# The values product of the mixers' attention, and its drain, put a quarter of a job later

## The chip, the cores and the metric

The kernel runs on one core of a Trainium2 chip. The metric is the device time of one execution in microseconds; the median of three runs of the kernel before is 2228.06 us (2226.67 to 2229.28).

## What is computed

Two networks follow each other on 256 rows of width 1024. The first block (dilated and block attention, a cross attention to a memory, a gated MLP with a short convolution) is not touched by the change. The second has two layers. Each layer's mixer takes a normalised input, multiplies it by one wide weight `w_in` and makes three branches of it: an attention, a gated spatial mix, and a convolution of 31 taps. Their gated sum is multiplied by `w_out`. The attention is this, eight query heads of width 128 on two key and value heads:

```python
def gqa_attend(q, k, v):
    s = jnp.einsum('bqhgd,bkhd->bhgqk', q, k).astype(jnp.float32) * ATTN_SCALE
    p = jax.nn.softmax(s, axis=-1).astype(v.dtype)
    return jnp.einsum('bhgqk,bkhd->bqhgd', p, v)
```

It runs three times: for the context rows in layer 0 (256 keys: "context mixer"), and for the main rows in layers 0 and 1 (512 keys, the context's and their own: "main mixers"). All inputs and outputs are float32, and weights are multiplied as a sum of two parts (below).

## The kernel before

**Jobs and quarters.** All weight products are cut into jobs: one job multiplies a 1024 x 512 piece of a weight by 256 rows, in four quarters of 256 weight rows. For each quarter SyncE loads the piece (`raw`), ScalarE (ACT) rounds it to `whi` (L1376), VectorE (DVE) writes the rest `wlo = raw - whi` (L1862), and TensorE (PE) multiplies: high by high, high by low and low by high, into the accumulator `gps` (two job-sized halves that alternate). Lines 1060 to 1062 are a job of the type with 512-wide products, 12 per quarter; lines 1067 to 1069 the other type. The split of quarter q of the next job waits until PE has used quarter q of this one (`used[q]`), so ACT and DVE work a whole job ahead of PE with the weights.

**Steps.** Everything else hangs on the jobs as steps. `put(job, q, kind, ...)` in `make_plan` hangs a step on quarter q of a job. Every engine walks the jobs in order, each quarter in order, and does its own part of each step. PE does the steps of a quarter, then the quarter's products. ACT and DVE do the steps of a quarter, then in the last quarter the job's evacuation from `gps`, then the split of the same quarter of the next job. DVE's steps of the kinds in `LATE` (among them `conv`, one tap of the convolution, four L1705, and `gv_rms`, ten short operations L1677 to L1429) come behind the split. Nothing is reordered at run time, so what stands first in an engine's list holds up what stands behind it.

**The attention in the mixer.** `hosts` in `mixer` names nine consecutive jobs (`ga1`, `gg1`, `gv0`, `gv1`, `gu0`, `gu1`, `gate0`, `gate1`, `branch0`). Job h of them takes the scores of head h, and finishes head h-1. The steps of one head are:

- `at`: PE's scores (L970, L971, in the context mixer L973) into banks 0 and 1 of `aps`; DVE's maximum (L1661, L1662).
- `atE`: ACT's exponential from the banks (L1206). `atR`: DVE's reciprocal of the sums (L1668). `atS`: ACT's scaling of the probabilities (L1215).
- `atT`: PE's transposes of them (L982) into banks 2 and 3 of `aps`, in the next job; ACT's copy to `PTb` (L1223).
- `atV`: PE's product of the values with `PTb` (L995), into bank 2 of `aps`. It waits for the copy.
- `atH`: ACT rounds the result out of bank 2 to `ohi` (L1227). `atL`: DVE writes the rest to `olo` (L1672). `atL` is the last reader of bank 2.

`use` keeps who has to be through with a bank before it is written again. For bank 2 after `atV` that is `atL` of the same head:

```python
            elif k == "atT":
                use(p, (2, 3), ("at_pt", p.of, 1, 1))
            elif k == "atV":
                use(p, (2,), ("at_lo", p.of, 1, 1))
```

and `atT` of the next head begins on PE with `free(p)`, which waits for it.

Of the kernel before, what the change touches and what calls it, by code (L numbers as in the profile page):

```python
# [41 lines left out]
HD2, QH, KVH = 128, 8, 2  # L42
# [57 lines left out]
def make_plan():  # L100
# [10 lines left out]
    def put(jb, q, kind, **args):  # L111
        p = Step(kind, **args)
        jb.aux[q].append(p)
        return p
# [141 lines left out]
    def mixer(l, s, t_h, slots, tab=None, kvc=None, first=None):  # L256
# [58 lines left out]
        hosts = [ga1, gg1, gv[0], gv[1], gu[0], gu[1], gates[0], gates[1], ba[0]]  # L315
        at, tq = [], [tq0]
        for h in range(QH + 1):

            t, e = (0, 1) if h > 1 else (1, 2)
            if h == 1:  # L320
                put(hosts[h], 0, "atR", of=at[0])
                put(hosts[h], 0, "atS", of=at[0])
            if h < QH:
                p = put(hosts[h], 0 if h else 2, "at", h=h, s=s, own=own, l=l, slot=a_, tk=tk, rq=tq[h // 4])
            if h:
                put(hosts[h], t, "atT", of=at[h - 1])
                put(hosts[h], e, "atV", of=at[h - 1])
                put(hosts[h], 2 if h < QH else 1, "atH", of=at[h - 1])
                put(hosts[h], (3 if h == 1 else 2) if h < QH else 1, "atL", of=at[h - 1])
            if h < QH:  # L330
                put(hosts[h], e if h else 3, "atE", of=p)
                if h:
                    put(hosts[h], 2 if h > 1 else 3, "atR", of=p)
                    put(hosts[h], 3, "atS", of=p)
                at.append(p)
            if h == 2:
                tq.append(put(gv[0], 3, "tq", of=rq1, banks=(0, 1)))
# [78 lines left out]
    t_next = prenorm(d1[1], 2, d2[0], 2, 0, "c", 0, "RA", 0, [("ctx_in", None, 0, 16), ("cp_done", j_q0, 1, 1)])  # L416
    put(d2[1], 1, "gb", src=("g_final",))
    J, co, wo = mixer(0, "c", t_next, (0, 1, 2))

    fin = Step("final", after={"act": [("res_done", d2[1], 1, 1)], "dve": [("res_done", d2[1], 1, 1)]})  # L420
# [8 lines left out]
    last_f2 = f2[-1]  # L429

    J, _, wo = mixer(0, "x", t_next, (2, 1, 0), tab, first=first)
    po_c = Step("po", res="c", wait=last_f2)
    J["kv"].aux[0].insert(0, po_c)
# [10 lines left out]
    f2[-1].then.append(po)  # L444
    t_next = prenorm(kvc, 1, kvc, 3, 1, "x", 0, "RB", 1, po=po)
    J, _, wo = mixer(1, "x", t_next, (1, 0, 2), tab, kvc)
    f10 = job("relu2", "ff11", 0, "W", 1, c=0, out=0)
    t = ffn(1, "x", f10, wo[1], 1, (0, 0, 0))
# [1480 lines left out]
```

## Time and profile before

| | before |
|---|---|
| median of 3 runs | 2228.06 us (2226.67 to 2229.28) |
| profiled execution, its own time | 2226.02 us |
| its span in the trace | 2224.2 us |
| mean granted TensorE clock over the span | 0.985 of full speed |
| PE busy | 2113.8 us (95%) |
| DVE busy | 1666.3 us (75%) |
| ACT busy | 1224.8 us (55%) |

The span runs from the first to the last instruction; the execution's own time is 1.8 us longer. In the rows of the timeline the columns are: start in us, length in us, engine, line, operation, what it writes and reads, and how many were merged; in brackets the idle time just before it on its engine, and what ended it. A wait row names who waited, for whom, the total in us, how often, and the longest. The three stretches of attention lie at about 612 to 733 us (context), 1156 to 1291 us (main, layer 0) and 1729 to 1864 us (main, layer 1).

### The profile page before, as it was taken

Reading aid. Unit: us, or ns where it says so; the run is one execution under the profiler, and the core shown is the slowest. Engines: PE = TensorE matmul, PEld = TensorE weight load, DVE = VectorE, ACT = ScalarE, POOL = GpSimd, SP = SyncE. Lnnn points to the kernel's source line nnn. Section 1 sums busy time; section 2 is a strip of 40 time slices with the busy share of each in tenths; the row PEclk is TensorE's granted clock in tenths of the full one; section 3 lists DMA queues with packets and bytes.
Section 4 is the critical chain, followed back from the end, with each engine's and each line's share of the span. In section 5 each row is a group of like instructions: output and inputs, shape, how many; then the busy total and the mean of one; then the engine's idle time right before and its main releaser. Section 6 shows DMA issues by size and latency. Waiting matters only on the chain.

```text
span 2224.2 us, 30895 instructions
## 1 busy us (share of the span) xinstructions
PE 2113.8 (95%) x12005; PEld 1841.2 (83%) x12005; DVE 1666.3 (75%) x2501; ACT 1224.8 (55%) x1651; POOL 58.8 (3%) x112
## 2 busy tenths in 40 slices
PE   7999989998999999999999999989999999998997
PEld 6777779896887887988887788789878878877996
DVE  6676667777778987766687898675687789976555
ACT  5555654555566446555556644554555675454543
POOL 3000000000000000000000000000000000000000
PEclk9999999999999999999999999999999999998999
DMA  7545775667645445677654444556555544444663
GB/s 254 182 156 181 236 257 169 223 216 227 206 144 159 134 142 161 199 231 242 204 187 133 139 135 143 177 175 191 174 174 171 152 133 133 151 161 143 189 187 117
DMA packets 203809, 394.31 MB, mean 177 GB/s; under 512 B 14007, under 2 KB 16563, under 8 KB 203664
## 3 DMA queue, kind: packets, MB, share of 16 engines
q1 hardware_dynamic: 198368, 381.74, 54.7%
q0 software_dynamic: 5296, 10.60, 1.6%
q8 instruction: 96, 1.57, 0.3%
q14 instruction: 49, 0.40, 0.1%
HBM read 390.98 MB, written 1.30 MB: 176 GB/s over the span
## 4 chain that ended last, share of the span: by engine, by line
PE 79%; DVE 9%; ACT 6%; issue 3%; DMA 2%; DVEq 0%; ACTq 0%
PE gps L1060 14%; PE gps L1062 14%; PE gps L1061 14%; PE gps L1067 9%; PE gps L1069 9%; PE gps L1068 9%; DVE wlo L1862 3%; ACT whi L1376 2%; PE aps L1019 2%; PE aps L864 2%; PE aps L995 1%; DMA raw<-ada_w 1%; PE aps L1026 1%; DVE Yc L1705 1%; PE gps L1054 1%
## 5 line engine op out<-in xcount | busy, mean ns | idle before, releaser
L1862 DVE TENSOR_TENSOR wlo<-raw,whi 128x1024 fp32r<-128x1024 f32 (+1 forms) x728 | 873.4, 1213 | 402.1 <-ACT whi L1376 398.8
L1376 ACT ACTIVATE whi<-raw 128x1024 fp32r<-128x1024 f32 (+1 forms) x728 | 756.6, 1049 | 625.8 <-PE gps L1062 360.7
L1060 PE MATMUL gps<-whi,ohi 128*128 128x512 f32 x1624 | 651.9, 401 | 9.6 <-DVE olo L1733 4.9
L1062 PE MATMUL gps<-whi,olo 128*128 128x512 f32 x1624 | 634.4, 391 | 0.0
L1061 PE MATMUL gps<-wlo,ohi 128*128 128x512 f32 x1624 | 634.0, 390 | 0.0
L1067 PE MATMUL gps<-ohi,whi 128*128 128x256 f32 x1760 | 503.8, 286 | 0.6 <-issue 0.5
L1068 PE MATMUL gps<-olo,whi 128*128 128x256 f32 x1760 | 498.5, 283 | 0.0
L1069 PE MATMUL gps<-ohi,wlo 128*128 128x256 f32 x1760 | 498.4, 283 | 0.0
L1060 PEld LDWEIGHTS gps<-whi,ohi 128*128 128x128 f32 x1624 | 306.3, 189 | 77.3 <-issue 9.7
L1062 PEld LDWEIGHTS gps<-whi,olo 128*128 128x128 f32 x1624 | 305.5, 188 | 65.6
L1061 PEld LDWEIGHTS gps<-wlo,ohi 128*128 128x128 f32 x1624 | 306.1, 188 | 61.3
L1067 PEld LDWEIGHTS gps<-ohi,whi 128*128 128x128 f32 x1760 | 337.6, 192 | 8.5 <-issue 5.5
L1068 PEld LDWEIGHTS gps<-olo,whi 128*128 128x128 f32 x1760 | 337.7, 192 | 0.7
L1069 PEld LDWEIGHTS gps<-ohi,wlo 128*128 128x128 f32 x1760 | 337.5, 192 | 0.0
L1705 DVE SCALAR_TENSOR_TENSOR Yc<-GLP,CW,Yc 128x256 f32<-128x256 f32 x612 | 252.7, 479 | 0.0
L1054 PE MATMUL gps<-whi,chi 128*128 128x512 f32 x192 | 81.4, 424 | 16.7 <-DVE wlo L1862 16.7
L1055 PE MATMUL gps<-wlo,chi 128*128 128x512 f32 x192 | 77.2, 402 | 0.0
L1054 PEld LDWEIGHTS gps<-whi,chi 128*128 128x128 f32 x192 | 37.5, 195 | 30.8 <-DVE wlo L1862 23.8
L864 PE MATMUL aps<-ident,RB 128*128 128x128 f32 x160 | 28.9, 348 | 32.4 <-DVE RB L1448 30.0
L1781 DVE TENSOR_TENSOR TT<-TT 128x1024 f32<-128x1024 f32 x24 | 29.4, 1226 | 37.3 <-ACT TT L1318 37.3
L864 PEld LDWEIGHTS aps<-ident,RB 128*128 128x128 f32 x160 | 24.6, 182 | 36.9 <-DVE RB L1448 33.8
L1206 ACT ACTIVATE Pb<-aps,den,st 128x512 f32<-128x512 f32 (+1 forms) x48 | 33.5, 703 | 32.4 <-DVE den L1662 32.4
(286 smaller groups left out, 1624.1 us busy)
## 6 DMA issues: line engine op xcount, KB each, us to landing
raw<-w_in SPq DMA_DIRECT2D x232, 512.0 KB, 3.8
raw<-w_ff SPq DMA_DIRECT2D x192, 512.0 KB, 4.1
raw<-ada_w SPq DMA_DIRECT2D x96, 512.0 KB, 4.8
raw<-w_out SPq DMA_DIRECT2D x32, 512.0 KB, 4.4
raw<-w_attn_o SPq DMA_DIRECT2D x24, 512.0 KB, 3.3
raw<-w_gmlp_o SPq DMA_DIRECT2D x24, 512.0 KB, 3.3
raw<-w_conv_o SPq DMA_DIRECT2D x24, 512.0 KB, 4.2
raw<-w_gate SPq DMA_DIRECT2D x20, 512.0 KB, 4.4
```

Of the source, the lines that this page charges most:

```text
L864: t = nc.tensor.transpose(aps[:, b, i * S + m * P:i * S + m * P + P], src[:, m, (2 * b + i) * P:(2 * b + i + 1) * P], ident[:])
L1054: mm(o[:, 0:NW], chi[:, k, :], whi[:, q, i, :], start=first, stop=False)
L1055: t = mm(o[:, 0:NW], chi[:, k, :], wlo[:, q, i, :], start=False, stop=last)
L1060: mm(om, ah, whi[:, q, i, :], start=first, stop=False)
L1061: mm(om, ah, wlo[:, q, i, :], start=False, stop=False)
L1062: t = mm(om, al, whi[:, q, i, :], start=False, stop=last)
L1067: mm(on, wh, ohi[:, jb.slot, k, :], start=first and n % 2 == 0, stop=False, skip_group_check=True)
L1068: mm(on, wh, olo[:, jb.slot, k, :], start=False, stop=False, skip_group_check=True)
L1069: t = mm(on, wl, ohi[:, jb.slot, k, :], start=False, stop=last, skip_group_check=True)
L1376: A_(part(whi, jb, q), part(raw, jb, q), ACT.Copy).then_inc(hi_done[q], 1)
L1705: stt(y, x, CW[:, p.l, tap * KT + k:tap * KT + k + 1], y, ALU.mult, ALU.add).then_inc(sem["cv_done"], 1)
L1862: tt(part(wlo, jb, q), part(raw, jb, q), f32(part(whi, jb, q)), ALU.subtract).then_inc(lo_done[q], 1)
```

## The change

Three entries of the table of steps get other quarters. The values product goes from quarter 1 to quarter 2 of its job, ACT's rounding and DVE's rest from quarter 2 to quarter 3. This holds for heads 1 to 6, which are finished in the jobs `gv0` to `gate1`. Head 0 (finished in `gg1`) had its product in quarter 2 already and its rest in quarter 3; only its rounding moves, from 2 to 3. Head 7 (finished in `branch0`) keeps its places. No operation is added or taken away, and no wait is changed.

```diff
             if h:
                 put(hosts[h], t, "atT", of=at[h - 1])
-                put(hosts[h], e, "atV", of=at[h - 1])
-                put(hosts[h], 2 if h < QH else 1, "atH", of=at[h - 1])
-                put(hosts[h], (3 if h == 1 else 2) if h < QH else 1, "atL", of=at[h - 1])
+                put(hosts[h], 2 if h < QH else 1, "atV", of=at[h - 1])
+                put(hosts[h], 3 if h < QH else 1, "atH", of=at[h - 1])
+                put(hosts[h], 3 if h < QH else 1, "atL", of=at[h - 1])
```

DVE in the context mixer, job `gv1`, from its second quarter's split to its evacuation (`L1752`); `L1862` is the split, `L1705` a tap, `L1672` the rest of the values product, `L1668` the reciprocal:

```order
 L1862 TENSOR_TENSOR wlo<-raw,whi 128x1024 x2
 L1705 SCALAR_TENSOR_TENSOR Yc<-GLP,CW,Yc 128x256 x4
-L1672 TENSOR_TENSOR olo<-aps,ohi 128x256
-L1668 RECIPROCAL den<-den 128x2
-L1862 TENSOR_TENSOR wlo<-raw,whi 128x1024
-L1705 SCALAR_TENSOR_TENSOR Yc<-GLP,CW,Yc 128x256 x4
+L1668 RECIPROCAL den<-den 128x2
+L1862 TENSOR_TENSOR wlo<-raw,whi 128x1024
+L1705 SCALAR_TENSOR_TENSOR Yc<-GLP,CW,Yc 128x256 x4
+L1672 TENSOR_TENSOR olo<-aps,ohi 128x256
 L1752 TENSOR_TENSOR TT<-TT,gps 128x1024
```

The rest, last reader of bank 2, now stands behind the third quarter's split and the tap that follows it; the reciprocal stands ahead of both without the rest before it.

ACT in the same job, from the scaling's predecessor to the evacuation (`L1206` exponential, `L1234` another step's squares, `L1376` the rounding of the weights, `L1240` the first tap, `L1227` the rounding of the values product, `L1215` the scaling, `L1298` the evacuation):

```order
 L1206 ACTIVATE Pb,den<-aps,den,st 128x256 x2
 L1234 ACTIVATE RB,st<-RA 128x512 x2
-L1376 ACTIVATE whi<-raw 128x1024
-L1227 ACTIVATE ohi<-aps 128x256
-L1376 ACTIVATE whi<-raw 128x1024
+L1376 ACTIVATE whi<-raw 128x1024 x2
 L1240 ACTIVATE Yc<-GLP,C,CW 128x256 x4
+L1227 ACTIVATE ohi<-aps 128x256
 L1215 ACTIVATE Pb<-Pb,den 128x256 x2
 L1298 ACTIVATE TT<-gps 128x1024
```

The rounding of the product goes behind the third quarter's rounding of weights, and stays ahead of the scaling. On PE the product passes the 12 weight products of the second quarter.

## Rows read from the trace of the kernel before

**Rows 1.** The page: busy time of each engine over the span.
```profile
PE 2113.8 (95%) x12005; PEld 1841.2 (83%) x12005; DVE 1666.3 (75%) x2501; ACT 1224.8 (55%) x1651; POOL 58.8 (3%) x112
```

**Rows 2.** Who waited for whom, PE alone: total, times, longest.
```profile
PE aps L995 <- ACT PTb L1223: 11.7, 10, 1.6
...
PE aps L982 <- ACT Pb L1215: 7.7, 8, 2.3
```

**Rows 3.** Timeline, PE, context mixer: transposes of heads 3 to 7, one product, one head's scores.
```profile
665.84 0.63 PE L982 MATMUL aps<-ident,Pb 128*128 128x128 f32 x4 [0.62 <-ACT Pb L1215]
...
670.80 1.10 PE L995 MATMUL aps<-PTb,kvb 128*128 128x256 f32 x4 [1.57 <-ACT PTb L1223]
...
680.81 0.60 PE L982 MATMUL aps<-ident,Pb 128*128 128x128 f32 x4
...
695.90 0.63 PE L982 MATMUL aps<-ident,Pb 128*128 128x128 f32 x4 [0.38 <-ACT Pb L1215]
...
709.94 1.02 PE L973 MATMUL aps<-kvb,qT 128*128 128x256 f32 x4
...
710.80 0.60 PE L982 MATMUL aps<-ident,Pb 128*128 128x128 f32 x4
...
723.28 0.63 PE L982 MATMUL aps<-ident,Pb 128*128 128x128 f32 x4
```

**Rows 4.** Timeline, PE, main mixer of layer 0: transposes of heads 3 to 7, first scores of head 7.
```profile
1215.73 1.06 PE L982 MATMUL aps<-ident,Pb 128*128 128x128 f32 x8
...
1232.86 1.04 PE L982 MATMUL aps<-ident,Pb 128*128 128x128 f32 x8
...
1248.83 1.06 PE L982 MATMUL aps<-ident,Pb 128*128 128x128 f32 x8
...
1264.13 0.59 PE L970 MATMUL aps<-kvb,qT 128*128 128x256 f32 x2
...
1265.86 1.04 PE L982 MATMUL aps<-ident,Pb 128*128 128x128 f32 x8
...
1280.02 1.07 PE L982 MATMUL aps<-ident,Pb 128*128 128x128 f32 x8 [0.48 <-ACT Pb L1215]
```

**Rows 5.** The rest of the values product by its line: ns of one (min/median/max).
```profile
L1672 DVE TENSOR_TENSOR olo<-aps,ohi x24: 412/417/421, 634.6 to 1861.6; 128x256 fp32r<-128x256 f32 x24
```

**Rows 6.** Timeline, DVE, context mixer: last work of the third quarter, heads 3 to 6.
```profile
665.79 1.67 DVE L1705 SCALAR_TENSOR_TENSOR Yc<-GLP,CW,Yc 128x256 f32<-128x256 f32 x4
...
681.69 0.16 DVE L1429 SCALAR_TENSOR_TENSOR st<-st 128x2 f32<-128x2 f32 x1
...
694.73 1.20 DVE L1862 TENSOR_TENSOR wlo<-raw,whi 128x1024 fp32r<-128x1024 f32 x1
...
710.68 1.66 DVE L1705 SCALAR_TENSOR_TENSOR Yc<-GLP,CW,Yc 128x256 f32<-128x256 f32 x4
```

**Rows 7.** The same for the main mixer of layer 0.
```profile
1215.05 1.67 DVE L1705 SCALAR_TENSOR_TENSOR Yc<-GLP,CW,Yc 128x256 f32<-128x256 f32 x4
...
1232.68 0.16 DVE L1429 SCALAR_TENSOR_TENSOR st<-st 128x2 f32<-128x2 f32 x1
...
1248.36 1.66 DVE L1705 SCALAR_TENSOR_TENSOR Yc<-GLP,CW,Yc 128x256 f32<-128x256 f32 x4
...
1264.30 1.67 DVE L1705 SCALAR_TENSOR_TENSOR Yc<-GLP,CW,Yc 128x256 f32<-128x256 f32 x4
```

**Rows 8.** Timeline, ACT, main mixer: second quarter's rounding in job `gu1`.
```profile
1241.81 1.06 ACT L1376 ACTIVATE whi<-raw 128x1024 fp32r<-128x1024 f32 x1 [0.43 <-PE gps L1062]
```

**Rows 9.** Timeline, ACT, job `gate1`: third quarter's rounding (context; main), scaling (main).
```profile
720.60 1.06 ACT L1376 ACTIVATE whi<-raw 128x1024 fp32r<-128x1024 f32 x1 [1.39 <-PE gps L1062]
...
1276.92 1.06 ACT L1376 ACTIVATE whi<-raw 128x1024 fp32r<-128x1024 f32 x1 [1.39 <-PE gps L1062]
...
1278.54 1.34 ACT L1215 ACTIVATE Pb<-Pb,den 128x512 f32<-128x512 f32 x2 [0.56 <-DVE den L1668]
```

**Rows 10.** A stretch by windows: length, PE, PEld, DVE, ACT, POOL busy, PEclk, DMA share, GB/s.
```profile
2015.00:2030.00 15.00, 4.53 (x20) 3.27 (x19) 10.84 (x28) 5.57 (x10) 0.53 (x1) 0.68 0.54 167
```

## The prediction

> **What bounds the kernel now.** I read the page first: PE is busy for 95% of the span [rows 1], so time comes only from PE's idle time or from other work on PE. Then the waits of PE alone [rows 2]: the values product waits 11.7 us in all for ACT's copy of the transposed probabilities, in ten places, and the transposes wait 7.7 us for ACT's scaling. Then the timeline around such a place. In job `gu0` of the context mixer the transposes start at 665.84 and the product at 670.80, after 1.57 us of idleness [rows 3]. The copy is late because ACT, behind the end of the previous job, has that job's evacuation ahead of it in its list. A product a quarter later would find the copy done. Four of the ten places lie in the context mixer and three in each main one.
>
> Last I read the transposes themselves, the place where one head hands over to the next. They need two things: the scaled probabilities, and bank 2 of `aps`, which the rest of the previous head's product (L1672) must have left. In the trace before, nobody waits for L1672, since it stands ahead of the reciprocal and the reciprocal ahead of the scaling, so it is always done first. That order is what the change gives up.
>
> **What the change removes.** With the product behind the second quarter's 12 weight products (about 2.7 us), all ten waits go: -11.7 us on PE, if nothing else held it. The reciprocal no longer has the 0.42 us of L1672 in front of it [rows 5] (about 0.33 net, because operations on DVE overlap a little), so the scaling can be up to 0.33 us earlier per job where DVE is what it waits for. The rounding on ACT keeps its length and only changes place; it is hidden where ACT idles for PE, as it did for 1.39 us before the rounding of weights in `gate1` [rows 9], and costs up to its 0.4 us where ACT has no slack (job `gv1`, where ACT goes from the weights to the first tap to the scaling). No DMA, SyncE or GpSimd instruction moves.
>
> **What it adds.** The rest now stands behind DVE's third-quarter split and whatever tap or statistics follow it. Its earliest end, counted from ACT's third rounding of weights, which itself waits for PE's third quarter: 1.06 (L1376 [rows 9]) + 1.20 (L1862 [rows 6]) + 1.67 (four L1705 [rows 6]) + 0.42 (L1672 [rows 5]) = 4.35 us; the hops between engines of some 0.1 us (the scaling ends at 1279.88 and the transposes start at 1280.02 [rows 9, 4]) are about made up by the overlap of consecutive DVE operations. PE, from the same moment, has the fourth quarter, 2.62 us (from 1276.92 to 1280.02 less its 0.48 of idleness [rows 9, 4]), and the next head's scores, 1.73 us in a main mixer (1264.13 to 1265.86 [rows 4]) and 0.86 us in the context mixer (709.94 to 710.80 [rows 3]), none before the last transposes. So even when DVE keeps up, PE waits about 0 us per head in the main mixers, 0.8 us in the context mixer, and 1.7 us at the last head of each. Where DVE is behind, it is more.
>
> **The sum, head by head.** The start of the transposes afterwards is the later of PE's arrival and the end of the rest. For the rest I take the end of the DVE work that now precedes it [rows 6, 7], add 0.45, and subtract how much earlier DVE gets there. If it were not earlier at all, the starts of heads 3 to 6 would be:
>
> - Context: 667.9, 682.3, 696.4, 712.8, against 665.84, 680.81, 695.90, 710.80 before [rows 3].
> - Main: 1217.2, 1233.3, 1250.5, 1266.4, against 1215.73, 1232.86, 1248.83, 1265.86 [rows 4].
>
> DVE's lead, from walking through its list and ACT's with the durations of the trace: 0.3 to 0.5 us for heads 3 to 5 of the context mixer and 0.85 us for head 6; in a main mixer 0.6 and 0.5 us for heads 3 and 4, then 1.55 us for heads 5 and 6, because in `gu1` the second rounding of weights waited for PE [rows 8], and PE gets there earlier without the product ahead of it. That gives shifts of the transposes against before of
>
> - context: +1.6, +1.2, 0, +1.15 us for heads 3, 4, 5, 6;
> - main: +0.9, -0.1, +0.1, -1.0 us.
>
> The last head decides, as PE's work behind it is unchanged and PE does not wait there. Its third quarter starts with the shift of head 6, and the transposes follow 4.35 us behind the rounding: context 720.60 + 4.35 = 724.95, main 1276.92 + 4.35 = 1281.27, which is 1.67 and 1.25 us behind the starts before. With head 6: context 1.15 + 1.67 = +2.8 us; main -1.0 + 1.25 = +0.25 us, twice. **Sum +3.3 us.** PE's waits by this: the 11.7 us at the product are gone, some 19 us appear at the transposes, for L1672.
>
> Bounds: the shift of head 6 lies between 0 (PE arriving as before, which the 0.8 us of wait per head nearly forbids) and +2.0 (DVE not earlier) in the context mixer, between -1.4 (PE never held) and +0.5 in a main one. So +1.7 to +3.7, and twice -0.15 to +1.75: +1.4 to +7.2 us. I take 3.3, nearer the low end, because DVE's lead is made of rows that really move up.
>
> Behind the attention DVE is busy without a gap up to the statistics of the convolution, but both engines enter that stretch shifted alike, so I add nothing for it. The granted clock adds noise: long idle stretches of PE, as in 2015 to 2030 us with PE busy for 4.53 of 15 us, are followed by half clock, 0.68 on average there [rows 10], and a shift of the program may lengthen or shorten such a piece; +-2 us.
>
> The profiled execution of 2226.02 us would become 2229.3 us; it lies 2 us under the median of the runs, so the median goes from 2228.06 to **2231.4 us**, +0.15%.
>
> **Rivals.** About 0.2% (4.5 us) is what a measurement of this kernel can tell from no change.
>
> 1. *The waits go and nothing takes their place*: -11.7 us at most. The same walk without the condition on bank 2 gives -1.5 us in the context mixer and twice -3.4 us, because the scaling then holds PE in part: -8.3 us, 2220 us. For it: the largest wait of the attention goes. Against it: `use` gives bank 2 to L1672, and the sum of four operations is longer than the fourth quarter in every one of the last heads. The Trainium skill, page Perfetto Trace Analysis, section Optimization Strategy, says to find the gaps of the engine in question and to make what they wait for start sooner or end faster; read with the wait list alone, this change answers it and would be worth the 11.7 us. Against that rule stands here that the gap is not removed but handed to another dependency. 8%.
> 2. *The forecast: no change that can be told, the sum above*: +1.4 to +4.4 us. 57%.
> 3. *Slower by more than 0.2%*: DVE is the bound of the attention, and its lead stays out. The place is the transposes of heads 3 to 7; if DVE is not earlier, head 6 stands at +2.0 and +0.5, which gives 3.7 + 2 x 1.75 = +7.2 us, 2235 us. It decides from a lead under about 0.4 us less per mixer than I took. For it: nothing in the trace shows how much DVE really gains when PE runs ahead of it, and the longest new wait is large: at head 3 of the context mixer PE arrived at 665.22 before, and by the same walk some 0.9 us earlier now, and is held till 667.4, some 3 us. Were the clock to fall there, the half speed of a few us comes on top. The page TensorE: Matmul & The Clock Gate of the Trainium skill (section Why this matters for your kernels) warns of idle gaps between bursts for this reason; the trace shows full clock over waits of up to 2.3 us in the attention [rows 2] and the half clock only behind longer idleness [rows 10], so 3 us is open. 32%.
> 4. *The product is not what is late*: the copy might still not be there a quarter later. The longest wait is 1.6 us [rows 2] and a quarter's products take 2.7 us, so this is nearly out; 3%, with no change in time.
>
> **The numbers.** The rivals of both signs beyond 0.2%: faster 0.08, slower 0.32; the rest, 0.60 (rivals 2 and 4), is within. The range takes in the bounds of the sum (+1.4 to +7.2 us) and the clock's noise on the low side: 2226.5 to 2236.5 us. It leaves rival 1 out.
>
> **What the changed profile would show.** L995 without idleness before it. L982 waiting for DVE `olo` L1672, about 19 us in 17 or so places, the longest about 3 us at head 3 of the context mixer; its waits for L1215 left only at head 1, where the longest of 2.3 us is. The last transposes of the context mixer about 2.8 us later than before, those of the main mixers 0 to 1 us further behind that. If the transposes wait for L1672 less than 12 us in all, the forecast is wrong towards rival 1; if more than 22 us, towards rival 3.

## The result and the profile after

| | before | after |
|---|---|---|
| median | 2228.06 us (15 runs, 2225.53 to 2234.25) | 2234.37 us (15 runs, 2230.01 to 2237.96) |
| ratio | | 1.0023, 95% interval 1.0014 to 1.0032 |
| profiled execution, its span | 2226.02, 2224.2 us | 2235.13, 2233.3 us |
| mean granted clock | 0.985 | 0.984 |

The change costs 3 to 7 us (the interval times 2228), 5.1 us at the ratio itself; the medians lie 6.3 us apart. A second measurement of the same program, `e8_after_again` below, gave 1.0019 [1.0007, 1.0031]. The predicted 2231.4 us is 3 us too low, and the measured value lies inside the range of 2226.5 to 2236.5 us, nearer its upper end.

The page, busy time over the span, to be held against [rows 1]:

```profile
PE 2119.5 (95%) x12005; PEld 1848.2 (83%) x12005; DVE 1667.2 (75%) x2501; ACT 1224.5 (55%) x1651; POOL 58.6 (3%) x112
```

The same 12005 matmuls are busy for 5.7 us longer. No instruction was added, so a share of PE's work ran slower. The list of PE's waits, against [rows 2]:

```profile
PE aps L982 <- DVE olo L1672: 16.9, 13, 3.0
...
PE aps L982 <- ACT Pb L1215: 5.8, 4, 2.3
```

L995 no longer waits. The 11.7 us before it are gone, and 16.9 us of waits for the rest L1672 stand before the transposes. Of the 7.7 us for the scaling L1215, the 5.8 us that remain are those of heads 0 and 1.

PE in the context mixer: the transposes of heads 0 and 3 to 7, and L1004, the first product of the spatial mix, which stands behind head 7 in `branch0` (against [rows 3]):

```profile
628.18 0.63 PE L982 MATMUL aps<-ident,Pb 128*128 128x128 f32 x4 [2.28 <-ACT Pb L1215]
...
670.36 0.66 PE L982 MATMUL aps<-ident,Pb 128*128 128x128 f32 x4 [2.98 <-DVE olo L1672]
...
686.52 0.66 PE L982 MATMUL aps<-ident,Pb 128*128 128x128 f32 x4 [1.19 <-DVE olo L1672]
...
700.08 0.66 PE L982 MATMUL aps<-ident,Pb 128*128 128x128 f32 x4 [0.22 <-DVE olo L1672]
...
716.16 1.12 PE L982 MATMUL aps<-ident,Pb 128*128 128x128 f32 x4 [2.74 <-DVE olo L1672]
...
731.80 0.66 PE L982 MATMUL aps<-ident,Pb 128*128 128x128 f32 x4 [1.67 <-DVE olo L1672]
...
741.40 0.81 PE L1004 MATMUL aps<-RA,wsT 128*128 128x256 f32 x3
```

The two ends of the same stretch in the kernel before:

```profile
625.05 0.63 PE L982 MATMUL aps<-ident,Pb 128*128 128x128 f32 x4 [2.27 <-ACT Pb L1215]
...
732.86 1.46 PE L1004 MATMUL aps<-RA,wsT 128*128 128x256 f32 x6
```

This distance, from head 0's transposes to L1004, is the measure used from here on, since nothing the change touches lies outside it and the three stretches start at times that vary. In the context mixer it was 732.86 - 625.05 = 107.81 us and is 741.40 - 628.18 = 113.22 us. Read in the same way, a main mixer was 120.90 us (both) and is 120.49 and 120.47 us. Head 0 itself comes 3.1 us later, ahead of everything the change touches: so much do two executions differ there.

What holds the transposes at 670.36 (timeline, DVE and ACT in job `gv1`):

```profile
667.11 0.16 DVE L1668 RECIPROCAL den<-den 128x2 f32<-128x2 f32 x1
667.16 0.37 ACT L1227 ACTIVATE ohi<-aps 128x256 fp32r<-128x256 f32 x1
667.18 1.21 DVE L1862 TENSOR_TENSOR wlo<-raw,whi 128x1024 fp32r<-128x1024 f32 x1
667.42 0.90 ACT L1215 ACTIVATE Pb<-Pb,den 128x256 f32<-128x256 f32 x2
668.30 1.67 DVE L1705 SCALAR_TENSOR_TENSOR Yc<-GLP,CW,Yc 128x256 f32<-128x256 f32 x4
669.88 0.42 DVE L1672 TENSOR_TENSOR olo<-aps,ohi 128x256 fp32r<-128x256 f32 x1
```

The probabilities were scaled at 668.32 and the product rounded at 667.53. On DVE the split (1.21) and the tap (1.67) stand between the rounding and the rest. That is the handing over which the prediction described.

Behind two of these waits PE runs at half clock. The windows behind the waits of 2.98 and 2.74 us (columns as in [rows 10]; the seventh number after the length is the granted clock):

```profile
670.00:675.00 5.00, 4.64 (x16) 3.74 (x17) 4.83 (x7) 2.81 (x4) 0.00 (x0) 0.66 0.46 139
...
716.00:724.00 8.00, 7.84 (x30) 6.57 (x31) 5.33 (x11) 2.87 (x7) 0.00 (x0) 0.79 0.33 114
```

Single products show the change of level (timeline, PE): they start 0.23 us apart at 2.4 GHz, and 0.43 us apart from 671.94 on.

```profile
671.32 0.40 PE L1062 MATMUL gps<-whi,olo 128*128 128x512 f32 x1
671.55 0.59 PE L1060 MATMUL gps<-whi,ohi 128*128 128x512 f32 x1
671.94 0.63 PE L1061 MATMUL gps<-wlo,ohi 128*128 128x512 f32 x1
672.37 0.63 PE L1062 MATMUL gps<-whi,olo 128*128 128x512 f32 x1
```

Such a piece costs 1.5 to 1.6 us: the clock is short of full speed by 0.34 x 5 = 1.7 us of clock time in the first window and 0.21 x 8 = 1.7 in the second, nearly all of it under busy PE. From head 3 to head 4 it is 686.52 - 670.36 = 16.16 us here and 14.56 us in a profile of the same program without the piece (below), from head 6 to head 7 15.64 and 14.16 us.

### The profile page after: what moved, and what is told of

Its sections match the earlier page's. It is cut to its first block, busy times and chain, and to the rows that moved or that the text cites. A ratio compares the mean times of both kernels' runs of the same rounds, so it can differ in the third digit from the quotient of the medians.

```text
span 2233.3 us, 30895 instructions
## 1 busy us (share of the span) xinstructions
PE 2119.5 (95%) x12005; PEld 1848.2 (83%) x12005; DVE 1667.2 (75%) x2501; ACT 1224.5 (55%) x1651; POOL 58.6 (3%) x112
## 4 chain that ended last, share of the span: by engine, by line
PE 75%; DVE 13%; ACT 7%; issue 3%; DMA 3%; DVEq 0%; ACTq 0%
PE gps L1060 13%; PE gps L1061 13%; PE gps L1062 13%; PE gps L1067 9%; PE gps L1068 9%; PE gps L1069 9%; DVE wlo L1862 4%; ACT whi L1376 3%; PE aps L1019 2%; DVE Yc L1705 2%; PE aps L864 2%; DMA raw<-ada_w 2%; PE aps L1026 1%; PE aps L995 1%; PE gps L1054 1%
## 5 line engine op out<-in xcount | busy, mean ns | idle before, releaser
L1862 DVE TENSOR_TENSOR wlo<-raw,whi 128x1024 fp32r<-128x1024 f32 (+1 forms) x728 | 873.8, 1213 | 414.0 <-ACT whi L1376 411.4
L1376 ACT ACTIVATE whi<-raw 128x1024 fp32r<-128x1024 f32 (+1 forms) x728 | 756.5, 1049 | 646.3 <-PE gps L1062 372.2
L1705 DVE SCALAR_TENSOR_TENSOR Yc<-GLP,CW,Yc 128x256 f32<-128x256 f32 x612 | 253.0, 482 | 0.0
L1019 PE MATMUL aps<-GLP,Pb 128*128 128x256 f32 x216 | 51.0, 378 | 0.0
```

The costliest lines, as they stand in the source:

```text
L1019: t = mm(aps[:, i // 2, (i % 2) * S:(i % 2 + 1) * S], Pb[:, p.of.n % 2, i * P:(i + 1) * P], GLP[:, 4 + i, p.of.tap:p.of.tap + S], start=p. ...
L1376: A_(part(whi, jb, q), part(raw, jb, q), ACT.Copy).then_inc(hi_done[q], 1)
L1705: stt(y, x, CW[:, p.l, tap * KT + k:tap * KT + k + 1], y, ALU.mult, ALU.add).then_inc(sem["cv_done"], 1)
L1862: tt(part(wlo, jb, q), part(raw, jb, q), f32(part(whi, jb, q)), ALU.subtract).then_inc(lo_done[q], 1)
```

## The experiments

Theory A: bank 2 is what the transposes wait for. The rest of the product, behind the third quarter's split and a tap, gives it back too late. Theory B: it is the product in its new place, or a later finish of `olo`, that costs. A second question is what the half clock adds. One table holds the stretches of all profiles; "pieces" counts the stretches at half clock within the context mixer's. The main mixers have none but where the table says so. Each kernel is held against the kernel before as measured beside it, whose median lies between 2227.5 and 2229.0 us.

| | ratio to before [95%] | context, pieces | main 0, main 1 |
|---|---|---|---|
| before | 1 | 107.81, 0 | 120.90, 120.90 |
| after | 1.0023 [1.0014, 1.0032] | 113.22, 2 | 120.49, 120.47 |
| after, measured again | 1.0019 [1.0007, 1.0031] | 111.70, 1 | 120.52, 120.54 |
| product moved alone | 0.9969 [0.9958, 0.9981] | 108.39, 2 | 118.09, 118.10 |
| rounding and rest moved alone | 1.0021 [1.0009, 1.0033] | 110.70, 0 | 121.99, 122.05 |
| context product in bank 3 | 0.9981 [0.9972, 0.9990] | 107.49, 2 | 120.45, 120.48 |
| 10 idle products | 1.0019 [1.0009, 1.0029] | 112.57, 0 | 120.45, 120.41 |
| 5 idle products | 1.0009 [0.9996, 1.0022] | 110.11, 0 | 120.52, 120.45 |
| third-quarter taps away | 1.0042 [1.0028, 1.0057] | 113.61, 3 | 124.47, 123.43 (one each) |
| all in quarter 2, rest behind reciprocal | 0.9956 [0.9940, 0.9973] | 107.20, 1 | 116.80, 116.78 |
| rest behind reciprocal alone | 0.9992 [0.9981, 1.0003] | 108.36, 1 | 119.86, 119.88 |
| the last but one, and head 0's wait filled | 0.9958 [0.9945, 0.9970] | 105.72, 0 | 116.79, 116.80 |

### The product alone

Against the changed kernel:

```diff
-                put(hosts[h], 3 if h < QH else 1, "atH", of=at[h - 1])
-                put(hosts[h], 3 if h < QH else 1, "atL", of=at[h - 1])
+                put(hosts[h], 2 if h < QH else 1, "atH", of=at[h - 1])
+                put(hosts[h], (3 if h == 1 else 2) if h < QH else 1, "atL", of=at[h - 1])
```

> The product a quarter later as in the change, its rounding (L1227) and rest (L1672) back in quarter 2, ahead of the reciprocal. Theory A (the late rest holds bank 2, and nothing else of the change costs): the product's wait for L1223 is 0 as after, the transposes' wait for L1672 is gone (16.9 us after), some of it is taken over by the scaling (L1215), net about -1.5 us in the context mixer and -3.4 us in each main one against before: about 2220 us. Rival B (it is the product's later place that costs): as after or worse, 2232 us or more, with waits for the product on ACT and DVE.

Measured: 2221.73 us against 2228.96, ratio 0.9969 [0.9958, 0.9981]. PE's waits at the transposes (this kernel's only row for L982, and none for L995):

```profile
PE aps L982 <- ACT Pb L1215: 13.2, 11, 2.3
```

So the product in its new place costs nothing. By itself it is worth 6.9 us (0.0031 x 2229), and L1672 is waited for by nobody. Where PE waits now, the scaling is what it waits for, the scaling waits for the reciprocal, and the rest stands in front of that (main mixer of layer 0, from the end of job `gu0` to the transposes of head 5):

```profile
1244.48 0.42 DVE L1672 TENSOR_TENSOR olo<-aps,ohi 128x256 fp32r<-128x256 f32 x1
1244.81 0.15 DVE L1668 RECIPROCAL den<-den 128x2 f32<-128x2 f32 x1
...
1245.00 1.33 ACT L1215 ACTIVATE Pb<-Pb,den 128x512 f32<-128x512 f32 x2 [3.05 <-DVE den L1668]
...
1246.48 1.06 PE L982 MATMUL aps<-ident,Pb 128*128 128x128 f32 x8 [1.24 <-ACT Pb L1215]
```

### The rounding and the rest alone

```diff
-                put(hosts[h], 2 if h < QH else 1, "atV", of=at[h - 1])
+                put(hosts[h], e, "atV", of=at[h - 1])
```

> The product in quarter 1 as before, only its rounding and rest late (quarter 3). Theory A: the transposes still wait for L1672, whose time hangs on PE's third quarter and DVE; the product's wait for L1223 is back in part; slower than before by 4 to 9 us, 2232 to 2237 us. Rival B (the product's place costs): no slower than before, 2226 to 2229 us.

Measured: 2233.84 us against 2228.96, ratio 1.0021 [1.0009, 1.0033]. Waits of PE:

```profile
PE aps L982 <- DVE olo L1672: 15.8, 13, 2.3
...
PE aps L995 <- ACT PTb L1223: 3.1, 4, 1.1
```

The loss is there although the product is early: its place does not matter to it, the rest's does. Of the copy's 11.7 us only 3.1 are left with the product where it was. The evacuation still stands ahead of the copy on ACT, but the transposes now come later against it: at head 3 of the context mixer the copy starts 2.7 us behind them (668.25 to 670.98), and 4.2 us in the kernel before (665.84 to 670.08). With the product late as well the total for L1672 is nearly the same, 16.9 us.

### Another bank for the product

In the context mixer the transposes fill bank 2 alone, so its product can go to bank 3 (in the main mixers they fill both). The same index changes in ACT's rounding and in the rest, the order of everything stays that of the changed kernel:

```diff
-                use(p, (2, 3), ("at_pt", p.of, 1, 1))
+                use(p, (2, 3) if p.of.s == "x" else (2,), ("at_pt", p.of, 1, 1))
...
-                use(p, (2,), ("at_lo", p.of, 1, 1))
+                use(p, (2,) if p.of.s == "x" else (3,), ("at_lo", p.of, 1, 1))
```

> The changed kernel, but in the context mixer the product goes into bank 3 of aps, which its four transposes leave free; nothing moves. Theory A: in the context mixer the transposes no longer wait for L1672 (8.8 us there after) and the two stretches of half clock in it go; the scaling holds PE for some of it; 5 to 8 us faster than after, about 2228 us; the main mixers keep 8.1 us of waits for L1672. If the bank is not the cause (DVE too late in general), the time stays within 2 us of after, 2234 us.

Measured: 2225.15 us against 2228.96, ratio 0.9981 [0.9972, 0.9990]. Waits of PE:

```profile
PE aps L982 <- ACT Pb L1215: 9.5, 7, 2.3
PE aps L982 <- DVE olo L1672: 8.1, 8, 1.7
```

The 8.1 us left are the two main mixers'. The rest is as late as before on DVE, and nobody in the context mixer minds: the bank is the cause. The context mixer takes 107.49 us, 5.7 less than in the profile of the changed kernel, with the same number of pieces at half clock. They did not go away as expected: they now lie behind the waits for the scaling at head 0 (2.27 us) and head 5 (1.93 us). The kernel is 9 us faster than the changed one (4.2 + 5.1), where 5 to 8 had been expected; the stretches account for 5.7 of that, and the rest is open.

### The waits filled

Does the half clock come from these waits? On PE, ahead of the transposes of heads 3 and 6 of the context mixer, products with no use into bank 3 keep it busy (10, then 5 in a second kernel):

```diff
             def atT(p):
-                free(p)
                 a = p.of
+                if a.s == "c" and a.h in (3, 6):
+                    wait(pe, p.bank_free[3])
+                    for _ in range(10):
+                        mm(aps[:, 3, 0:S], ident[:], kvb[:, a.own, 0:S], start=True, stop=True)
+                free(p)
```

> The changed kernel with ten more products of 128x256 (identity with keys, into the unused bank 3, nobody reads them) on PE ahead of the transposes of heads 3 and 6 in the context mixer, inside the two longest waits. Theory A with the clock: the transposes start no earlier, their waits there shrink from 3.0 and 2.7 us to under 1 us, no half clock behind them, and the kernel is 3 us faster than after (1.5 us per stretch) though PE does more: 2231 us. If the half clock does not come from these waits: two stretches of half clock remain and the time stays at 2234 us or more.

Measured: 2233.05 us against 2228.96, ratio 1.0019 [1.0009, 1.0029]. No piece at half clock in the context mixer, but ten took over 4 us and outlasted the waits (heads 3 and 6 stand at 43.35 and 88.88 us behind head 0, against 42.17 and 86.36 with five). So it could not tell the price of the clock. Five:

> As e4_fill with five products instead of ten, which lasted 4.2 us there and so outlasted the waits of 3.0 and 2.7 us by 1.2 and 1.5 us. Theory A with the clock: the waits at heads 3 and 6 of the context mixer shrink to 0.9 and 0.6 us, no half clock behind them, the stretch from the first transposes of the context mixer to the spatial product is 3 us shorter than after (113.2 us), 110.2 us. Rival: a remaining wait still brings the half clock, 113 us.

Measured: 2230.96 us against 2227.54, ratio 1.0009 [0.9996, 1.0022]. PE at heads 3 and 6:

```profile
668.90 0.66 PE L986 MATMUL aps<-ident,Pb 128*128 128x128 f32 x4 [0.84 <-DVE olo L1676]
...
713.09 0.65 PE L986 MATMUL aps<-ident,Pb 128*128 128x128 f32 x4 [0.57 <-DVE olo L1676]
```

The context mixer takes 110.11 us: 3.1 less than in the profile of the changed kernel, with over 4 us more of PE's work. That is the price of its two pieces, and 110.1 - 107.8 = 2.3 us is what the order costs there without them. The time alone doesn't show the gain: 2.0 us over the kernel before has an interval of -0.9 to +4.9 us, which overlaps that of the changed kernel.

### The changed kernel again

> The changed kernel once more, for a second profile. The waits for L1672 must be the same to 0.1 us each (16.9 us in all). If the half clock follows from the waits of 2.98 and 2.74 us, both stretches are there again and the context mixer takes 113.2 us from its first transposes to the spatial product; if it is chance, one or both are missing and it takes 111.7 or 110.2 us.

Measured: 2233.19 us against 2227.54, ratio 1.0019 [1.0007, 1.0031]. PE at heads 3 and 6:

```profile
672.51 0.66 PE L982 MATMUL aps<-ident,Pb 128*128 128x128 f32 x4 [3.06 <-DVE olo L1672]
...
716.71 0.66 PE L982 MATMUL aps<-ident,Pb 128*128 128x128 f32 x4 [2.73 <-DVE olo L1672]
```

and the windows behind both (this profile's head 3 lies 2.2 us later than the other's, so its stretch takes a second window):

```profile
670.00:675.00 5.00, 2.49 (x13) 2.15 (x14) 4.82 (x9) 4.50 (x7) 0.00 (x0) 1.00 0.57 177
675.00:686.00 11.00, 10.87 (x49) 8.68 (x47) 8.28 (x19) 7.97 (x16) 0.00 (x0) 1.00 0.45 133
...
716.00:724.00 8.00, 7.29 (x34) 6.14 (x35) 6.81 (x14) 4.21 (x8) 0.00 (x0) 1.00 0.41 139
```

The same program with the same waits has full clock behind both. Its only piece lies behind the wait of 2.27 us at head 0, which the kernel before has too. So a wait of 2 to 3 us brings the half clock in one execution and not in another. Without their pieces, 113.22 - 3.0 and 111.70 - 1.5, both profiles give 110.2 us, as the five idle products did.

This also says that two waits filled and no piece behind them prove little by themselves, since here the same waits stayed unfilled with no piece either. Over all twelve profiles the three attention stretches have 24 unfilled waits of 1.9 us or more at the transposes, with a piece behind 14 of them and no piece anywhere else; the five filled ones (two each in the kernels with 10 and 5 products, and one in the last kernel below) have none.

### The taps out of the rest's way

Theory A puts 1.67 us of tap in front of the rest. Here the third-quarter taps of the host jobs go behind the fourth quarter's split:

```diff
-                    put(J[name], q, "conv", half=half, l=l, of=cv0[half], taps=[tap])
+                    put(J[name], 3 if q == 2 and J[name] in hosts[:QH] else q, "conv", half=half, l=l, of=cv0[half], taps=[tap])
```

> The changed kernel with the convolution's taps that follow the third quarter's split in the eight attention jobs put behind the fourth quarter's, so that only the split (and, in gu0, the statistics) stands ahead of L1672. Theory A (L1672's time is the sum of what stands ahead of it on DVE): the rest ends 1.6 us earlier at heads 3, 6 and 7, and the transposes' waits for L1672 fall from 16.9 us to about 6, mostly at the head of gu0 (1.2 us context, 0.9 us main, nothing moved there); the last wait of each mixer falls from 1.67 to about 0.1 us; 5 us faster than after, 2229 us. Rival B (the product's late place or the bank itself, not what is ahead of the rest): the waits stay, 2234 us.

Measured: 2236.34 us against 2227.54, ratio 1.0042 [1.0028, 1.0057]. The expectation missed. The waits at the last heads did fall (1.67 to 0.78 us in the main mixers), but the total for L1672 stayed at 17.0 us, and main 0 grew by 4.0 us, main 1 by 3.0. DVE at the turn from `gv1` to `gu0` in the main mixer of layer 0, this kernel:

```profile
1229.50 3.25 DVE L1705 SCALAR_TENSOR_TENSOR Yc<-GLP,CW,Yc 128x256 f32<-128x256 f32 x8
1232.67 1.22 DVE L1661 TENSOR_REDUCE den<-aps 128x2 f32<-128x1024 f32 x1
```

and the changed one:

```profile
1229.51 1.67 DVE L1705 SCALAR_TENSOR_TENSOR Yc<-GLP,CW,Yc 128x256 f32<-128x256 f32 x4
1231.09 1.22 DVE L1661 TENSOR_REDUCE den<-aps 128x2 f32<-128x1024 f32 x1
```

The second tap delays head 4's maximum by 1.58 us, with it the exponential, the job's splits, the reciprocal and at last the rest (1242.26 against 1240.69): PE waits 3.3 us at head 4 instead of 0.87. The tap in front of the rest had only been pushed in front of something tighter. DVE does idle for 2.74 us in that job, but behind the maximum, ahead of the second quarter's split at 1236.38.

Much of the growth is the clock. Behind the wait at head 4 PE runs at half clock in both main mixers, for less than 4 us in main 1 and about 7 us in main 0, where the level falls while PE still waits:

```profile
1240.00:1242.00 2.00, 0.00 (x0) 0.00 (x0) 1.72 (x10) 1.97 (x4) 0.00 (x0) 0.88 0.73 232
```

The transposes of head 5 follow those of head 4 by 17.98 us in main 0 and 16.92 us in main 1, so the longer piece costs 1.1 us more, about 2.5 us. Without these two pieces each main mixer grows by 1.5 us, which is about the 1.58 us of the tap, and the context mixer without its three is 1.1 us shorter than the changed kernel's.

### All in the second quarter, the rest behind the reciprocal

The product alone had left the rest in front of the reciprocal. This kernel keeps product, rounding and rest in quarter 2 and puts the rest of heads 1 to 6 behind the reciprocal of the next head:

```diff
-                put(hosts[h], 3 if h < QH else 1, "atH", of=at[h - 1])
-                put(hosts[h], 3 if h < QH else 1, "atL", of=at[h - 1])
+                put(hosts[h], 2 if h < QH else 1, "atH", of=at[h - 1])
+                if h in (1, QH):
+                    put(hosts[h], 3 if h == 1 else 1, "atL", of=at[h - 1])
...
                     put(hosts[h], 3, "atS", of=p)
+                if h > 1:
+                    put(hosts[h], 2, "atL", of=at[h - 1])
```

> Product, rounding and rest in quarter 2 as in e1_product_only, but the rest (L1672) behind the reciprocal, ahead of the third split. The scaling no longer waits for the rest: 0.33 us earlier per job where DVE is what it waits for. Against e1_product_only the waits of the transposes for L1215 (13.2 us in all) fall by 1 to 2 us, and the time by 1 to 2 us, 2220 us; if the rest ahead of the reciprocal costs nothing, it is 2221.7 us as there.

Measured: 2219.10 us against 2227.54, ratio 0.9956 [0.9940, 0.9973]. It beats both kernels, by 9.8 us (0.0044 x 2228) against before. Waits of PE (three lines longer, so L985 is the transposes):

```profile
PE aps L985 <- ACT Pb L1218: 12.3, 10, 2.3
```

Bank 2 comes free ahead of the third split and tap, and the scaling is the only thing the transposes wait for. Against the product alone these waits fall by 0.9 us, a little less than the 1 to 2 expected; each main mixer is 1.3 us shorter, and by the ratios the kernel gains 2.9 us. The reciprocal's share, alone, on the kernel before (product back in its first quarter):

> Theory A (the order on DVE decides, and what PE waits for last in each job is what a shorter chain can give back): the product is back in the first quarter, only the rest stands behind the reciprocal, still in the second quarter. With the product early, PE waits for the scaling for only about 2 us in all beyond head 0 (7.7 in all, 5.7 of them at head 0, which the edit does not touch), so the reciprocal 0.33 us earlier per job gives at most that: 2226 to 2227 us against 2227.5 to 2228 of the kernel before (ratio 0.9990 to 0.9997). PE: the product waits 11 to 13 us for the copy, the transposes 6 to 7 us for the scaling, none for the rest. Rival (the two edits are worth a fixed amount each and add up): the kernel with both gained 8.4 us, the product alone 7.2, so 1.2 us remain for the reciprocal; the timeline of the two mains, 1.3 us shorter each with both edits, would rather give 2.6 us or more: 2225 us.

Measured: 2227.05 us against 2228.12, ratio 0.9992 [0.9981, 1.0003]. The median agrees with theory A, but the interval, -4.2 to +0.7 us, holds the rival's 2225 as well. The stretches shorten by 1.0 us in each main mixer and, less one piece at half clock, 0.95 us in the context mixer, 3 us in all, which speaks for the rival: more than the 2 us of waits for the scaling which theory A gave as the most. The waits show what theory A left out. In the main mixer of layer 0 of the kernel before and of this one, PE waits for ACT's copy of the transposed queries as well:

```profile
PE aps L970 <- ACT qT L1190: 0.6, 1, 0.6
...
PE aps L973 <- ACT qT L1193: 0.4, 1, 0.4
```

This wait, at the scores of head 3, falls by 0.2 to 0.3 us, the waits for the copy by 0.2 (3.4 to 3.2) and those for the scaling by 0.3 (2.1 to 1.8), together most of the 1.0 us. Whether the time falls by 1 or 3 us is left open. The two edits about add up: 6.9 and 1.8 us alone, 9.8 us together.

### Head 0's wait filled

Five products of the same kind at the wait of head 0 of the context mixer, `a.h == 0`, on top of the kernel above:

> The clock: the kernel with product, rounding and rest in the second quarter (rest behind the reciprocal), and 5 idle products (ident by kvb into bank 3, some 2.1 us, results overwritten) ahead of the wait of 2.28 us at the transposes of head 0 of the context mixer; nothing else is changed. If idleness there calls the half clock: the granted clock stays 1.0 over the following 16 us, head 1's transposes come 11.1 to 11.3 us behind head 0's instead of 12.64, the context mixer takes 105.5 to 105.9 us instead of 107.20 although PE has more to do, and the median is 2217 to 2218.5 us. If the half clock there is chance or comes from something earlier in the program, it comes back in this run or in some: context 107.2, median 2219 to 2220.

Measured: 2219.12 us against 2228.12, ratio 0.9958 [0.9945, 0.9970]. PE, here:

```profile
625.83 2.32 PE L984 MATMUL aps<-kvb,ident 128*128 128x256 f32 x10
628.25 0.63 PE L989 MATMUL aps<-ident,Pb 128*128 128x128 f32 x4
...
639.40 0.63 PE L989 MATMUL aps<-ident,Pb 128*128 128x128 f32 x4 [0.17 <-ACT Pb L1222]
```

and in the kernel above without them:

```profile
627.02 0.63 PE L985 MATMUL aps<-ident,Pb 128*128 128x128 f32 x4 [2.28 <-ACT Pb L1218]
...
639.66 0.52 PE L985 MATMUL aps<-ident,Pb 128*128 128x128 f32 x3 [0.17 <-ACT Pb L1218]
```

Head 1 follows 11.15 us behind head 0 instead of 12.64, and the stretch takes 105.72 us instead of 107.20: as expected. The median is not 1 us lower as expected, but the same (five runs each), and so is the span, 2217.3 us in both. This profile's head 0 comes 1.2 us later and the part between the two main mixers takes 1.1 us more (452.82 against 451.76), and why was not followed up. A saving of 1.5 us can be seen in the stretch and not in the time.

## Why the prediction was right, and where not

**The waits at the product go.** Right: none of 11.7 us is left.

**They return at the transposes for L1672.** Right in kind. Forecast were about 19 us in 17 places with 3 us at head 3 of the context mixer; measured were 16.9 in 13, with 2.98 there. In a main mixer only heads 3, 4, 5 and 7 wait. The waits for L1215 that are left are at heads 0 and 1, the 2.3 us at head 0 and not at head 1 as the prediction has it. The bank experiment shows that the wait is for the bank.

**4.35 us from the third rounding to the end of the rest, 1.7 us of wait at each last head.** Right. In `gate1` of the main mixer of layer 0 (timeline):

```profile
1283.66 1.06 ACT L1376 ACTIVATE whi<-raw 128x1024 fp32r<-128x1024 f32 x1 [3.40 <-PE gps L1062]
...
1285.89 1.66 DVE L1705 SCALAR_TENSOR_TENSOR Yc<-GLP,CW,Yc 128x256 f32<-128x256 f32 x4
1287.48 0.41 DVE L1672 TENSOR_TENSOR olo<-aps,ohi 128x256 fp32r<-128x256 f32 x1
1287.94 1.09 PE L982 MATMUL aps<-ident,Pb 128*128 128x128 f32 x8 [1.67 <-DVE olo L1672]
```

From 1283.66 to 1287.94 it is 4.28 us.

**The sum, head by head.** The step that was off is DVE's lead. Measured from head 0, and with 1.5 us taken off behind each piece at half clock, the shifts of heads 3, 4, 5, 6 and 7 in the context mixer are +1.4, +1.1, -0.4, +0.7, +2.4 us (forecast +1.6, +1.2, 0, +1.15, +2.8), and in a main mixer +0.7, -0.1, -0.1, -1.7, -0.4 us (forecast +0.9, -0.1, +0.1, -1.0, +0.25). At head 6 of the context mixer DVE got there 0.4 us earlier than its walked list said. In the main mixers nothing holds PE at head 6, and its transposes start 0.7 us earlier than forecast, earlier than even the bound of -1.4. The last head's own term was right within 0.04 us. The order alone is thus +2.4 - 0.4 - 0.4 = +1.6 us, not +3.3.

**The clock.** This is the other term that was mis-sized. The prediction put it as noise of 2 us to either side and named the fall at head 3 only within rival 3. The profile of the changed kernel has two pieces, 1.5 us each, directly behind the new waits of 2.98 and 2.74 us. With five idle products in those waits both are gone and the context mixer is 3.1 us shorter, though the second profile lacks them without any products. That the half clock comes from such waits rests on the count over all profiles (14 of 24 unfilled, 0 of 5 filled); what decides it from one execution to the next is open. The page TensorE: Matmul & The Clock Gate of the Trainium skill (section Why this matters for your kernels) warns of idle gaps between bursts; here gaps of 1.9 to 3.1 us were followed by half clock in some executions and not in others. The 2.74 us at head 6 were not foreseen: the forecast's 0.8 us per head left out how much earlier PE arrives.

**The whole.** +1.6 us of order and 1.5 to 3.0 us of clock make +3.1 and +4.6 us in the two profiles' stretches, against +4.2 and +5.1 us by the ratios. The missing 0.5 to 1 us is within what executions differ by: the part between the two main mixers, where every kernel here has the same steps, takes 451.4 to 453.3 us in the twelve profiles. That the measured median lies within 3 us of the forecast is in part luck, since 1.7 us too much for the order stands against 1.5 to 3 us too little for the clock. The kernel before may also run with a piece behind its own wait of 2.27 us at head 0 more often than its one profile shows; this was not counted.

**The rivals.** Rival 1, that the waits go and nothing replaces them, needs the rest to stay early: the product moved alone shows its 8.3 us nearly (6.9). Between the forecast and rival 3 the result stands on the edge: 1.0023 and 1.0019, with intervals that hold 1.002. Of the two brackets, +1.4 to +4.4 us at 57% and more at 32%, the first measurement (+5.1) falls into rival 3's and the second (+4.2) into the forecast's. Rival 3's own mechanism, DVE's lead staying out, is refuted: head 6 stands at +0.7 and -1.7 us, not at +2.0 and +0.5. Its aside about the clock is what happened. Rival 4 is refuted, since L995 waits for nothing.

**The range.** It is about 1 us wider on either side than the parts it is said to be made of: 2228.06 + 1.4 - 2 and 2228.06 + 7.2 give 2227.5 to 2235.3 us. The measured 2234.37 lies inside this too.

## What to carry to other kernels

Ask of every wait removed who has to wait for what was moved with it: a drain is also the release of a buffer, and belongs as early as its input allows, or into a buffer of its own; here the move of the product was worth 6.9 us, and with its drain moved too the kernel lost 4 to 5 us. Look at what stands ahead of the operation that the critical chain really needs (the reciprocal, not the rest). And where a new wait of 2 to 3 us appears on PE, price the half clock behind it as a term with a chance, not as noise.

## What was not expected of the hardware

The same wait of 2.27 us at head 0 of the context mixer was followed by a piece at half clock in six of the eleven profiles that have it unfilled, and by full clock in five, under programs that hardly differ up to there; in the one profile in which it was filled, by full clock. Waits of 1.9 to 2.0 us at head 5 were followed by one in two profiles (the product alone, bank 3) and not in two others (the last two kernels with everything in quarter 2). A piece in the context mixer costs 1.5 to 1.6 us, whichever wait it follows. One piece is longer: with the taps away, the wait of 3.31 us in the main mixer of layer 0 has about 7 us of half clock behind it, which costs about 2.5 us.
